# Output projection of the last phase as three products of rounded halves, the state decay on the turned keys, and single buffers

## What is computed

```python
u, w = sol[..., :dv], sol[..., dv:]
v_new = u - jnp.einsum('bhck,bhkv->bhcv', w, S)
attn = jnp.einsum('bhik,bhjk->bhij', qc, kc) * decay
o = jnp.einsum('bhck,bhkv->bhcv', qc * jnp.exp(gcum)[..., None], S) + jnp.einsum('bhij,bhjv->bhiv', attn, v_new)
S = S * jnp.exp(g_last)[..., None] + jnp.einsum('bhck,bhcv->bhkv', kc * jnp.exp(g_last - gcum)[..., None], v_new)
...
o = (head_rmsnorm(o) * gn_w).reshape(B, L, O_MIX) * jax.nn.silu(z)
out = o @ w_out
return h + out.astype(h.dtype), s_gdn_new, xp[:, -(GDN_CONV - 1):]
```

## Time and profile before

| | us |
|---|---|
| median of 3 runs | 3436.76 |
| lowest, highest | 3436.21, 3436.82 |
| the profiled execution | 3444.35 |
| its span, first to last instruction | 3442.5 |
| mean granted TensorE clock of it | 0.95 |
| the odd mixing part in it, from its first transfer | 2563 to 3442 |

### The profile page before, as it was taken

One profiled execution on the slowest core, in us unless ns is written; L12 is line 12 of the kernel. 1 busy time (PEld: TensorE's weight loads), 2 busy tenths in 40 slices (PEclk: granted clock), 3 DMA queues, 4 the chain that ended last, 5 costly groups with the idle time before them and its releaser, 6 DMA issues. The chain is left out here.

```text
span 3442.5 us, 88583 instructions
## 1 busy us (share of the span) xinstructions
PE 3218.3 (93%) x38630; PEld 2732.1 (79%) x38630; DVE 1832.0 (53%) x3672; ACT 989.9 (29%) x2216; POOL 596.4 (17%) x549
## 2 busy tenths in 40 slices
PE   8999999958999999999969999999977999999997
PEld 8999999956776767677649999999966776776774
DVE  4212223225665655656445257667755677777754
ACT  4211111113332323333028222222223333333320
POOL 0000000012332323333210000000002222222211
PEclk9999999976999999999889999999987999999988
DMA  5222112132111212121043222112132122222221
GB/s 158 92 71 71 64 66 70 55 118 77 56 49 60 72 37 72 37 72 60 26 137 110 83 68 73 62 70 71 61 99 91 51 76 76 76 72 73 75 94 74
DMA packets 194449, 255.95 MB, mean 74 GB/s; under 512 B 29968, under 2 KB 161296, under 8 KB 193808
## 3 DMA queue, kind: packets, MB, share of 16 engines
q1 hardware_dynamic: 184272, 218.23, 19.7%
q0 software_dynamic: 9792, 32.06, 3.0%
HBM read 156.68 MB, written 93.55 MB: 73 GB/s over the span
## 5 line engine op out<-in xcount | busy, mean ns | idle before, releaser
L1370 PE MATMUL me_b<-me_w_out,me_mixT 128*128 128x512 f32 x544 | 281.7, 645 | 0.0
L2411 PE MATMUL mo_b<-mo_w_out,mo_mixT 128*128 128x512 f32 x544 | 261.0, 614 | 0.8 <-ACT mo_mixT L2014 0.8
L350 DVE SCALAR_TENSOR_TENSOR po_stage<-po_work,po_cw,po_stage 128x424 f32<-128x424 f32 (+1 forms) x360 | 232.0, 644 | 27.9 <-issue 1.3
L462 PE MATMUL po_ps<-po_xnT_hi,po_w_hi 128*128 128x424 f32 x960 | 205.0, 355 | 0.0
L462 PE MATMUL po_ps<-po_xnT_hi,po_w_lo 128*128 128x424 f32 x960 | 204.4, 355 | 0.0
L462 PE MATMUL po_ps<-po_xnT_lo,po_w_hi 128*128 128x424 f32 x960 | 204.1, 354 | 0.0
L462 PEld LDWEIGHTS po_ps<-po_xnT_hi,po_w_hi 128*128 128x128 f32 x960 | 180.2, 188 | 5.2
L462 PEld LDWEIGHTS po_ps<-po_xnT_hi,po_w_lo 128*128 128x128 f32 x960 | 180.4, 188 | 4.5
L462 PEld LDWEIGHTS po_ps<-po_xnT_lo,po_w_hi 128*128 128x128 f32 x960 | 180.2, 188 | 4.6
L259 ACT ACTIVATE po_work<-po_ps 128x424 f32<-128x424 f32 (+1 forms) x120 | 61.6, 514 | 408.0 <-PE po_ps L462 408.0
L2411 PEld LDWEIGHTS mo_b<-mo_w_out,mo_mixT 128*128 128x128 f32 x544 | 98.0, 191 | 93.2 <-issue 87.5
(11 more groups left out here) (390 smaller groups left out, 6777.0 us busy)
## 6 DMA issues: line engine op xcount, KB each, us to landing
mo_c<-scratch_ch_o SPq DMA_DIRECT2D x51, 512.0 KB, 4.1
scratch_ch_o<-po_stage SPq DMA_DIRECT2D x96, 212.0 KB, 1.9
scratch_tok_e<-pe_stage SPq DMA_DIRECT2D x136, 128.0 KB, 1.9
pe_raw<-in_w_in_e POOLq DMA_DIRECT2D x56, 256.0 KB, 4.1
me_xs<-scratch_ch_e SPq DMA_DIRECT2D x17, 832.0 KB, 5.8
po_raw<-in_w_in_o POOLq DMA_DIRECT2D x48, 256.0 KB, 3.8
scratch_ch_e<-pe_stage SPq DMA_DIRECT2D x52, 212.0 KB, 1.9
scratch_tok_o<-po_stage SPq DMA_DIRECT2D x68, 130.0 KB, 1.7
```

The lines of the kernel that those rows point to most:

```text
L350: return nc.vector.scalar_tensor_tensor(out=o, in0=a, scalar=s, in1=b, op0=op0, op1=op1)
L462: last = nc.tensor.matmul(out, left.bitcast(F32R), right.bitcast(F32R), start=(i == 0 and k == 0), stop=(i == 2 and k == KD - 1))
L1370: return nc.tensor.matmul(o, l, r, start=start, stop=stop)
L2411: return nc.tensor.matmul(o, l, r, start=start, stop=stop)
```

## The change

1. **Projection.** `w_out` is kept as two tensors, `w_hi` (rounded) and `w_lo` (rest), and the turned mixed rows as `mixT` (rounded) and `mixT_lo`. Each product of a part becomes three of type F32R: 48 instructions a tile instead of 16 products of two instructions each.
2. **Splitting the weights.** `w_out` is loaded in eight slices into buffers that are not in use yet (`raw_w`). ACT rounds each slice, POOL subtracts. Four slices are done in the step m = 0, four in the step m = 1. The first use of each borrowed buffer waits for it: DVE's `solved(0)`, ACT's `scale_queries(0)` and SP's loads of h and the second gates wait for all eight.
3. **Splitting the mixed rows.** Behind ACT's rounding copy, DVE subtracts (`split_mix`), ahead of `solved` in its order; PE's part 0 waits for it.
4. **Decay on the keys.** The factor of `Wd` goes onto the turned keys: ACT writes them head by head with a scale (8 instructions instead of 2), DVE's `Wd` product goes, and `state_delta` reads `Wv`.
5. **Single buffers.** `o1`, `IL` and `TF` are single now, which makes room for the second weight tensor. `scale_queries(t)` waits for `mixed(t - 1)`. One of the sample states is loaded into `Wd` instead of `IL`, so later.
6. **Order on PE.** Part 6 goes from behind X64 to the end of the step, ahead of part 7.

```diff
@@ buffers @@
-        w_out = sb("w_out", [P, KD, D])
+        w_hi = sb("w_hi", [P, KD, D])
+        w_lo = sb("w_lo", [P, KD, D])
...
+        raw_w = [flat(AT[1]), flat(Wv), flat(Wd), mix[:], flat(o1), h_sb[0][:], h_sb[1][:], z[1][:]]
...
+        WEIGHTS_AT = {(0, None): (0, 1, 2, 3), (1, None): (4, 5, 6, 7)}
@@ SP @@
-            sp.dma_start(w_out[:], t_in["w_out_o"]).then_inc(s_w, 16)
-            for n in range(2):
-                load_z(n)
-                load_h(n)
+            for k in range(KD):
+                sp.dma_start(raw_w[k], t_in["w_out_o"][:, k, :]).then_inc(s_w[k], 16)
+            load_z(0)
             for o, p, t, n, m in STEPS:
+                if t == 0:
+                    sp.wait_ge(s_ws, KD)
+                    load_h(0)
+                    load_h(1)
+                    load_z(1)
@@ POOL @@
+            def split_weights(k):
+                pool.wait_ge(s_wh, k + 1)
+                nc.gpsimd.tensor_tensor(w_lo[:, k, :].bitcast(F32R), raw_w[k], w_hi[:, k, :], ALU.subtract).then_inc(s_ws, 1)
...
                     scale_values(m)
+                for k in WEIGHTS_AT.get((m, t), ()):
+                    split_weights(k)
@@ ACT @@
             def scale_queries(t):
                 await_(act, "qs_ready", t)
-                await_(act, "mixed", t - 2)
+                await_(act, "mixed", t - 1)
+                if t == 0:
+                    act.wait_ge(s_ws, KD)
...
-                A(mixT[:, 0:4, :], heads(bk[BC[0]], P), ACT.Copy)
-                A(mixT[:, 4:8, :], heads(bk[BC[1]], P), ACT.Copy).then_inc(E["mixT_written"], 1)
+                for half in range(2):
+                    last_op = A(mixT[:, 4 * half:4 * half + 4, :].bitcast(F32R), heads(bk[BC[half]], P), ACT.Copy)
+                last_op.then_inc(E["mixT_rounded"], 1)
...
-                A(tokK[m % 2][:, 0:4, :], heads(bk[BA[0]], P), ACT.Copy)
-                A(tokK[m % 2][:, 4:8, :], heads(bk[BA[1]], P), ACT.Copy)
+                for h in range(H):
+                    A(tokK[m % 2][:, h, :], head(BA, h), ACT.Copy, scale=Scales(m).edl[:, h:h + 1])
@@ DVE @@
+                if t == 0:
+                    dve.wait_ge(s_ws, KD)
...
-                tt(Wd[:], Wv[:], bc(s_.edl, GD), M).then_inc(E["wd_ready"], 1)
+            def split_mix(p):
+                await_(dve, "mixT_rounded", p)
+                for half in range(2):
+                    part = slice(4 * half, 4 * half + 4)
+                    last_op = tt(mixT_lo[:, part, :].bitcast(F32R), heads(bk[BC[half]], P), mixT[:, part, :], SU)
+                last_op.then_inc(E["mixT_written"], 1)
@@ PE @@
-                    last_op = mm(head(BA, h), tokK[t % 2][:, h, :], Wd[:, h, :])
+                    last_op = mm(head(BA, h), tokK[t % 2][:, h, :], Wv[:, h, :])
...
-                    last_op = mm(bk[BC[q]][:], mixT[:, k, :], w_out[:, k, q * 512:(q + 1) * 512], start=(k == 0), stop=(k == KD - 1))
+                    for i, (left, right) in enumerate(((mixT, w_hi), (mixT, w_lo), (mixT_lo, w_hi))):
+                        last_op = mm(bk[BC[q]][:], left[:, k, :].bitcast(F32R), right[:, k, q * 512:(q + 1) * 512].bitcast(F32R),
+                                     start=(k == 0 and i == 0), stop=(k == KD - 1 and i == 2))
```

More of the change, by code:

```diff
@@ L1798, in mix_odd_phase @@
         tokV = [sb(f"tokV{j}", [P, H, GD]) for j in range(2)]
-        o1 = [sb(f"o1_{j}", [P, H, GD]) for j in range(2)]
+        o1 = sb("o1", [P, H, GD])
         st = sb("st", [P, 2 * H + 3])
@@ L1804, in mix_odd_phase @@
         AT = [sb(f"AT{j}", [P, H, P]) for j in range(2)]
-        IL = [sb(f"IL{j}", [P, H, P]) for j in range(2)]
+        IL = sb("IL", [P, H, P])
         ILc = sb("ILc", [P, H, Q])
@@ L1810, in mix_odd_phase @@
         X64 = sb("X64", [P, H, 2 * Q])
-        TF = [sb(f"TF{j}", [P, H, P]) for j in range(2)]
+        TF = sb("TF", [P, H, P])
         Wv = sb("Wv", [P, H, GD])
@@ L1816, in mix_odd_phase @@
         mixT = sb("mixT", [P, KD, P])
+        mixT_lo = sb("mixT_lo", [P, KD, P])
         def flat(ap):
@@ L1849, in mix_odd_phase @@
         s_c = sem("constants_loaded")
-        s_w = sem("output_weights_loaded")
+        s_w = [sem(f"output_weights{k}_loaded") for k in range(KD)]
+        s_wh = sem("output_weights_rounded")
+        s_ws = sem("output_weights_split")
         s_in = {what: [sem(f"{what}{j}_loaded") for j in range(2)] for what in ("queries", "keys", "values")}
@@ L1989, in scale_values @@
                 mul(v[:], v[:], bc(Scales(m).root[:, 8:16], GD)).then_inc(E["values_scaled"], 1)
-            for j in range(2):
-                nc.gpsimd.memset(TF[j][:], 0.0)
+            def split_weights(k):
+                pool.wait_ge(s_wh, k + 1)
+                nc.gpsimd.tensor_tensor(w_lo[:, k, :].bitcast(F32R), raw_w[k], w_hi[:, k, :], ALU.subtract).then_inc(s_ws, 1)
+            nc.gpsimd.memset(TF[:], 0.0)
             nc.gpsimd.memset(TB[:], 0.0)
@@ L2025, in write_mixT, with round_weights @@
                 await_(act, "projected1", p - 1)
-                A(mixT[:, 0:4, :], heads(bk[BC[0]], P), ACT.Copy)
-                A(mixT[:, 4:8, :], heads(bk[BC[1]], P), ACT.Copy).then_inc(E["mixT_written"], 1)
+                for half in range(2):
+                    last_op = A(mixT[:, 4 * half:4 * half + 4, :].bitcast(F32R), heads(bk[BC[half]], P), ACT.Copy)
+                last_op.then_inc(E["mixT_rounded"], 1)
+            def round_weights(k):
+                act.wait_ge(s_w[k], 16)
+                A(w_hi[:, k, :].bitcast(F32R), raw_w[k], ACT.Copy).then_inc(s_wh, 1)
             def level(n, b):
@@ L2050, in square_outputs @@
                 await_(act, "o_summed", t)
-                await_(act, "state_delta_ready" if t < PT else "u1_ready", t)
-                A(osq(t)[:], o1[t % 2][:], ACT.Square).then_inc(E["o_squared"], 1)
+                await_(act, "stats_ready", t - 1)
+                await_(act, "u1_ready", t)
+                A(osq(t)[:], o1[:], ACT.Square).then_inc(E["o_squared"], 1)
             def decays(m):
@@ L2085, in final_root @@
                 await_(act, "h_ready", p)
-                A(flat(mixT), h_sb[p % 2][:], ACT.Square, accum_out=fs[:, 0:1])
+                A(flat(mixT).bitcast(F32R), h_sb[p % 2][:], ACT.Square, accum_out=fs[:, 0:1])
                 act.drain()
@@ L2136, in _ @@
                     level(n, 64)
+                for k in WEIGHTS_AT.get((m, t), ()):
+                    round_weights(k)
         @block.vector
@@ L2358, in _ @@
                     mask(n, 2)
+                if p is not None:
+                    split_mix(p)
                 if t is not None:
@@ L2447, in solve @@
                     for h in range(4 * q, 4 * q + 4):
-                        last_op = mm(head(BA, h), TF[t % 2][:, h, :], tokV[t % 2][:, h, :])
+                        last_op = mm(head(BA, h), TF[:, h, :], tokV[t % 2][:, h, :])
                     last_op.then_inc(E[f"u{q}_ready"], 1)
@@ L2638, in _ @@
                     level_X(n, 64)
-                if p is not None and p < PT:
-                    project(p, 6)
                 if m is not None:
```

39 lines of the change are left out of this document (21 added, 18 removed).

## The result

| | median of runs, us | against the kernel before (95%) |
|---|---|---|
| kernel before, 5 runs | 3436.76 | |
| changed kernel, 5 runs | 3458.58 | 1.0059 (1.0038 to 1.008) |
| changed kernel once more, 5 runs | 3457.38 (before: 3436.47, 20 runs) | 1.0063 (1.0051 to 1.0076) |

The forecast was 3447.9 with a range of 3435 to 3457. The direction was right (slower), the size was not: +21.8 instead of +11.1 (+20.9 when it was run again), and 1.6 us beyond the range.

A forecast was written before the change was run, and what follows sets the result against it. PE was taken to bound each step only up to the decay sums, then ACT, POOL and DVE. Loop +0.8, t = 1 -0.7, start +12.3, end -1.3 sum to +11.1 on 3436.8: 3447.9 us, range 3435 to 3457.

The forecast's parts named there:

- longer key copies in the empty step: ACT's eight scaled key copies cost about 1.1 us more, behind the exponential with ACT 35% busy; counted as nothing.
- first four subtractions: On POOL ahead of `mask_g(1)`, 2.30 us each, delaying PE's decay sums of m = 1: +4.4 us.
- second four, with the clock behind them: On POOL, holding up ACT's `scale_queries(0)` and level 2 copy, plus 0.5 for PE's low clock: +7.9 us.
- step t = 1 to t = 2: ACT's copy came before T2 was over, so half of the hand-over hides in t = 1: -0.7 us.
- thirteen steps of the loop: Each step: +1.40 for splitting mixed rows, less 2 x 0.67 for cheaper parts 0 and 1; +0.8 us in all.
- last steps: In the last step eight cheaper parts save 2.6 us, less 1.3 for the split ahead of the first: -1.3 us.
- ACT is 35% busy: Busy share cited to show that ACT's longer key copies, about 1.1 us more, cost nothing.
- PE is the bound after all: Rival: POOL and DVE start earlier whenever PE does, about 2.4 us gained per tile, total 3411 us; chance 0.08.
- The clock falls: Rival: PE idles more, so products with S slow by 1.6 us in 13 steps, +21, 3469 us; chance 0.08.
- Small gains cancel the start: Rival: products of 0.213, POOL subtractions of 1.85 or half the end's bound, any two giving 3437 to 3443; chance 0.20.
- the rival by the formula: PE products at the skill's 0.216 us: +4.5, 3441.3 us; chance within the 0.20 of small gains that cancel the start.
- The subtraction's cost is hidden: Rival: POOL's subtraction would cost nothing if `mask_g` stood ahead of it, which the order denies; no chance stated.

The follow-up runs named there:

- before_again: Kernel before, no edit, profiled a second time: phase 869.9 us, one execution 3438.22 us.
- before_third: Kernel before, no edit, profiled a third time: phase 869.9 us, one execution 3437.53 us.
- keys_scaled_only: Kernel before with only the decay moved onto the key copies, no `Wd`, projection still in f32: median 3439.16 us (0.9997 to 1.0017).
- masks_first: Changed kernel with POOL making the next tile's masked gates ahead of the four weight subtractions in both steps: median 3454.54 us (1.0041 to 1.0069).
- after: The changed kernel itself, first profile: phase 891.9 us, median 3458.58 us (1.0059).
- by_halves: Changed kernel with the rounded copy and remainder of the turned rows handed over in two halves: period 43.38 us, median 3440.13 us.
- part3_late: Changed kernel with projection part 3 behind X16, DVE's first-half addition behind the level 16 mask: period 43.11 us, median 3437.95 us.
- split_on_dve: Changed kernel with the eight weight subtractions on DVE instead of POOL, ACT rounding all pieces: phase 873.0 us, median 3442.89 us (1.0006 to 1.0028).

## Why the forecast was right in kind and too small

By its own terms, against before_again and before_third. The terms of the start are differences of single profiles, which scatter by 2 us and more:

| term | forecast | measured | from |
|---|---|---|---|
| longer key copies in the empty step | 0 | +4.0 | right side of t = 0 in keys_scaled_only and masks_first, 78.2 against 74.2 |
| first four subtractions | +4.4 | +5.9 | 84.1 - 78.2 |
| second four, with the clock behind them | +7.9 | +11.1 | 51.0 against 40.4 and 39.4 from t = 0 to t = 1 |
| step t = 1 to t = 2 | -0.7 | -1.5 | 44.5 against 45.3 and 46.9 |
| thirteen steps of the loop | +0.8 | +0.3 | 578.4 against 578.1 |
| last steps | -1.3 | +2.1 | 133.9 against 131.9 and 131.6 from the right side of t = 15 |
| sum | +11.1 | +22 | |

- **The loop was right, and for the reason given.** 0.233 for 0.231, 1.27 for 1.40, no gain from parts 4 to 7, the copy that ends with POOL. The formula of the Trainium skill named in the forecast ("TensorE: Matmul & The Clock Gate", section "Back-to-back issue gap"), 0.216 at the full clock, is not met by these products; the measured 0.233 decides, and it was the row at 424 columns that carried over. For the lower clock the same section of the Trainium skill gives N/1.2, which is 0.427 at 512 columns. The trace agrees: in the last step the products of part 1 start 0.427 apart (3398.10, 3398.53, 3398.95).
- **The step that failed** is the sentence "The median of the runs lies 7.6 below that execution, so the forecast is 3436.8 + 11.1". It takes for granted that the changed kernel's usual execution would be below its profile by as much. That execution had lost 9.4 us in the phase to a low clock at its start and its end, the places where the change now makes PE wait, and the changed kernel's phase repeats at 891.9 and 891.7. (Its two profiles do lie 5.4 and 6.3 above their medians, but these executions were late before the phase began, at 2570.3 and 2570.2.) In the terms of the start it went in a second time: "It did attend there at the low clock anyway, 3.47 us", so only 0.5 was added. Both later profiles of before do attend in 2.05, and the changed kernel takes 3.78. Against its own profile the forecast of +11.1 met 12.6; against the later ones the change costs 22. That 12.6 lies so near is partly luck: by the same terms it is +7.0 up to the right side of t = 0 (forecast 4.4), +8.9 to t = 1 (7.9), -2.4 to t = 2 (-0.7), +0.1 in the loop (+0.8) and -1.0 behind it (-1.3), so that larger gains behind the start made up for a part of what the start was forecast too low.
- **"ACT is 35% busy" was the wrong cover.** That share is from the full loop. In the first step the pipeline is empty and ACT's key copies are the path there. Their 1.1 became up to 4.0 at the right side of t = 0, where the clock fell behind the longer wait, and 1.2 at POOL's scaled values in the one profile where it didn't. POOL's queue starts later by that, not only by 4 x 2.30. As said above, it is not shown how much of this term lasts to the end. The subtraction itself was priced well: 2.35 to 2.40 for 2.30.
- **The last steps** lose instead of gaining. The waits of the window from 3386 to 3436 of after, and of the same window of before_again, 24 us earlier (engine, what waits, for whom: us, times, longest):

```profile
PE mo_b L2452 <- DVE mo_h L2168: 2.6, 1, 2.6
PE mo_b L2449 <- DVE mo_mixT_lo L2168: 1.9, 1, 1.9
```

```profile
PE mo_b L2414 <- DVE mo_h L2141: 1.4, 1, 1.4
PE mo_b L2411 <- ACT mo_mixT L2014: 0.6, 1, 0.6
```

  PE waits 2.5 us longer, and behind the 1.9 six products of part 1 start 0.43 apart instead of 0.233, 1.2 us more. That is 1.1 more than the 2.6 that the eight parts give. Another 0.4 to 0.8 lies in the step ahead, from the right side of t = 15 to that of the sample tile (59.3 against 58.9 and 58.5), which the forecast put at nothing. PE waits 1.55 us there for `mixT_lo`. The rest wasn't traced.
- **The rivals.** "PE is the bound after all" is refuted as it was put: the cheaper parts 4 to 7 gave nothing. It holds for the first stretch alone, where `by_halves` gave 1.08 of the 1.10 us of waiting that it took away and `part3_late` 1.35 of 1.40. "The clock falls" is refuted as it was put, for each step of the loop: there the clock stayed at 1.00 in the 500 us from 2770.3 on. It did fall at the start, where the forecast gave it 0.5 us, and in the last steps, where it gave it nothing. "Small gains cancel the start" needed products of 0.213 or subtractions of 1.85; they measured 0.233 and 2.35 to 2.40. For the rival by the formula the forecast has -3.0 at the end; by its own rule it is 8 x 0.42 - 1.3, a gain of 2.1, which makes 3442.2 instead of 3441.3. "The subtraction's cost is hidden" could have been true: `masks_first` hides the first four, `split_on_dve` all eight. The stated bounds above the forecast add up to 3455.9, not 3457; the result lies beyond both.

What stays open is how much of the 11.1 is the clock alone: the run that kept PE busy moved the low stretch instead of removing it. Open, too, is what makes the median of `split_on_dve` 6.4 above the kernel before when its profiled phase is only 3.1 longer.
